# Three modulation pieces, one weight remainder and the reload of x in another place on their queues

## The reference

```python
def first_block(x, ...):
    a = rms_norm(h, g_mix_pre)
    proj = a @ w_in
    attn = moba_attention(q, k, v)
    conv = conformer_conv(u, b_glu, w_dw, b_dw, ln_g, ln_b)   # depthwise, layer_norm over channels, silu
    mixed = concatenate([attn, conv], axis=-1) @ w_out
    h = h + rms_norm(mixed, g_mix_post)
    f = rms_norm(h, g_ffn_pre)
    f = square(relu(f @ w_ff1)) @ w_ff2
    h = h + rms_norm(f, g_ffn_post)

def _modulation(cvec, w, b):          # w is 2048 x 6144: shift, scale, gate
    m = silu(cvec) @ w + b
```

## Time and profile before

| | |
|---|---|
| median of 3 runs | 1825.3 us (1824.86 to 1826.06) |
| the profiled execution | 1826.15 us, its span 1824.4 us |
| TensorE busy | 1802.3 us, 99% |
| VectorE busy | 1468.7 us, 81% |
| ScalarE busy | 902.9 us, 49% |
| granted TensorE clock, mean | 0.998 |
| moved by DMA | 426.92 MB, 234 GB/s |

### The profile page before, as it was taken

One profiled execution on the slowest core, in us unless ns is written; L12 is line 12 of the kernel. 1 busy time (PEld: TensorE's weight loads), 2 busy tenths in 40 slices (PEclk: granted clock), 3 DMA queues, 4 the chain that ended last, 5 costly groups with the idle time before them and its releaser, 6 DMA issues.

```text
span 1824.4 us, 26132 instructions
## 1 busy us (share of the span) xinstructions
PE 1802.3 (99%) x9884; PEld 1558.2 (85%) x9884; DVE 1468.7 (81%) x1709; ACT 902.9 (49%) x1176; POOL 112.9 (6%) x217
## 2 busy tenths in 40 slices
PE   8999999999999999999999999999999999999998
PEld 7899987888888888888888888888888888888986
DVE  6899998878888897889887888746788778897854
ACT  6444566555434433553454557423656545445443
POOL 0000000000000000000000000000111010000000
PEclk9999999999999999999999999999999999999999
DMA  8756447777786787778977964654666784878562
GB/s 324 257 175 199 153 155 289 260 242 270 255 286 232 256 291 233 246 260 290 253 246 264 319 226 162 230 185 140 230 199 216 266 289 149 272 247 278 195 218 106
DMA packets 191016, 426.92 MB, mean 234 GB/s; under 512 B 12480, under 2 KB 12864, under 8 KB 189760
## 3 DMA queue, kind: packets, MB, share of 16 engines
q1 hardware_dynamic: 158560, 323.74, 52.3%
q0 software_dynamic: 27648, 100.68, 16.6%
q10 hardware_dynamic: 4704, 1.07, 0.3%
HBM read 421.23 MB, written 4.21 MB: 233 GB/s over the span
## 4 chain that ended last, share of the span: by engine, by line
PE 93%; DVE 4%; ACT 1%; DMA 1%; issue 1%; DVEq 0%; SPq 0%; POOLq 0%; ACTq 0%
PE banks L2073 23%; PE banks L2118 14%; PE banks L2120 14%; PE banks L2119 14%; PE banks L2079 12%; PE banks L2064 4%; PE banks L2066 4%; PE banks L2065 4%; PE banks L2419 2%; PE banks L2435 2%; PE banks L2182 1%; PE banks L2410 1%; DMA mod_raw<-in_ev_mod_w 1%; DVE w_lo L1146 1%; DMA scratch<-in_x 0%
## 5 line engine op out<-in xcount | busy, mean ns | idle before, releaser
L550 ACT ACTIVATE w_hi<-raw 128x1024 fp32r<-128x1024 f32 x552 | 579.5, 1058 | 658.3 <-PE banks L2120 333.5
L1146 DVE TENSOR_TENSOR w_lo<-raw,w_hi 128x1024 fp32r<-128x1024 f32 x552 | 667.1, 1222 | 244.0 <-ACT w_hi L550 241.8
L2073 PE MATMUL banks<-a_pair,w_hi 128*128 128x512 f32 x1792 | 431.2, 391 | 1.5 <-DVE a_pair L1276 0.8
L2073 PEld LDWEIGHTS banks<-a_pair,w_hi 128*128 128x128 f32 x1792 | 328.3, 188 | 65.2 <-issue 2.0
L2118 PE MATMUL banks<-w_hi,b_hi 128*128 128x512 f32 x808 | 317.0, 392 | 2.9 <-DVE w_lo L1392 2.6
L2120 PE MATMUL banks<-w_hi,b_lo 128*128 128x512 f32 x808 | 315.1, 390 | 0.0
L2119 PE MATMUL banks<-w_lo,b_hi 128*128 128x512 f32 x808 | 315.1, 390 | 0.0
L1186 DVE SCALAR_TENSOR_TENSOR mod_sum<-mod_raw,silu_c,mod_sum 128x1024 f32<-128x1024 f32 x240 | 302.9, 1283 | 12.1 <-DMA mod_raw<-in_ev_mod_w 8.3
L2079 PEld LDWEIGHTS banks<-a_pair,w_lo 128*128 128x128 f32 x1792 | 230.2, 191 | 8.8
L2079 PE MATMUL banks<-a_pair,w_lo 128*128 128x256 f32 x1792 | 234.6, 283 | 0.0
L2118 PEld LDWEIGHTS banks<-w_hi,b_hi 128*128 128x128 f32 x808 | 152.1, 188 | 35.8 <-issue 3.9
(11 more groups left out here) (249 smaller groups left out, 1684.5 us busy)
## 6 DMA issues: line engine op xcount, KB each, us to landing
raw<-in_w_ff SPq DMA_DIRECT2D x128, 1024.0 KB, 6.5
mod_raw<-in_ev_mod_w POOLq DMA_DIRECT2D x96, 512.0 KB, 5.3
mod_raw<-in_od_mod_w POOLq DMA_DIRECT2D x96, 512.0 KB, 5.1
raw<-in_ev_w_in SPq DMA_DIRECT2D x40, 1024.0 KB, 5.1
raw<-in_w_in SPq DMA_DIRECT2D x39, 1024.0 KB, 5.1
raw<-in_od_w_in SPq DMA_DIRECT2D x32, 1024.0 KB, 6.4
raw<-in_w_out SPq DMA_DIRECT2D x16, 1024.0 KB, 5.4
raw<-in_ev_w_out SPq DMA_DIRECT2D x16, 1024.0 KB, 6.6
```

The costliest lines, as they stand in the source:

```text
L550: nc.scalar.activation(w_hi[:, s % SLOTS], raw[:, s // 2, KPS * (s % 2):KPS * (s % 2) + KPS, :], ACT.Copy).then_inc(hi_ready, 1)
L1146: nc.vector.tensor_tensor(w_lo[:, s % SLOTS], raw[:, s // 2, KPS * (s % 2):KPS * (s % 2) + KPS, :], w_hi[:, s % SLOTS].bitcast(F32), ALU.s ...
L2073: e = nc.tensor.matmul(out[:, f, :], w_hi[:, s % SLOTS, t, P * f:P * (f + 1)], rows[:, :, KPS * s + t, :], start=s == 0 and t == 0, stop=F ...
```

## The change

On VectorE's queue, pieces 8 and 9 of `ev_gate` no longer stand between the squares' sum and the variance, and piece 10 no longer stands behind the last channel tile. Pieces 8 to 11 now follow remainders 40, 41, 42 and 43; pieces 12 to 14 follow 45 to 47, 15 to 17 follow 49 to 51, and 18 to 20 follow 53 to 55. Before, pieces 11 and 12 followed 41 and 43, 13 and 14 followed 45 and 47, 15 and 16 followed 49 and 51, and 17 to 20 followed 52 to 55. The remainder 35 moves from behind the scaling to the place between reciprocal and scaling. On SP's queue the reload of x is issued behind unit 13 instead of unit 11. No instruction is added or removed.

```diff
@@ -404,7 +404,7 @@
-                if u == 11:
+                if u == 13:
                     sp.wait_ge(conv_ready, 8)
                     sp.dma_start(X, tok(io["x"])).then_inc(x_in, 16)
@@ -1456,15 +1456,14 @@
             channels_added(conv_sq, square_total)
-            halves("ev_gate", 8, 2)
             dve.wait_ge(ln_sum, 2)
             nc.vector.tensor_scalar(ln_rstd[:], ln_var, 1.0 / 1024, LN_EPS, ALU.mult, ALU.add).then_inc(ln_act, 1)
             ahead1(34)
             dve.wait_ge(conv_sq_ready, 2)
             link(nc.vector.reciprocal(ln_rstd[:], ln_rstd[:]))
+            ahead1(35)
             nc.vector.tensor_tensor(conv_y, conv_y, ln_rstd[:].unsqueeze(1).to_broadcast([P, CONV_TILES, T]),
                                     ALU.mult).then_inc(ln_act, 1)
-            ahead1(35)
             ahead1(36)
@@ -1472,7 +1471,6 @@
                 if k in (0, 2, 5):
                     ahead1({0: 37, 2: 38, 5: 39}[k])
-            halves("ev_gate", 10, 1)
@@ -1492,13 +1490,13 @@
             for i in range(3):
                 for f in range(40 + 4 * i, 44 + 4 * i):
                     ahead1(f)
-                    if f % 2:
-                        halves("ev_gate", 11 + 2 * i + f % 4 // 2, 1)
+                    if f == 40 or f % 4:
+                        halves("ev_gate", 8 + f - 40 - i, 1)
                 gained(2 * i, i, out_acc[i])
             for f in range(52, 58):
                 ahead1(f)
-                if f < 56:
-                    halves("ev_gate", 17 + f - 52, 1)
+                if 52 < f < 56:
+                    halves("ev_gate", 18 + f - 53, 1)
```

## The result

The changed kernel takes 1831.69 us (median of 7 runs, 1830.45 to 1833.84), the one before 1824.92 beside it (7 runs, 1824.57 to 1826.06). The ratio is 1.0038, with a 95% interval of 1.0027 to 1.0050: slower by 6.8 us. The profiled execution has 1831.19 us and a span of 1829.5, 5.1 more than the 1824.4 of before; it is one of the faster ones of this kernel, and that of before was, at 1826.15, above all seven of its own.

A forecast was written before the change was run, and what follows sets the result against it. Bound by VectorE's layer-norm chain, then modulation loads. Step 12's gain of 0.4 to 2.1 us is lost and the chain ends 5.9 us later: median 1825.3 becomes 1831.2, range of 8 in 10 1826.0 to 1836.5.

The forecast's parts named there:

- What bounds: Output product: VectorE's layer-norm chain to about 296, modulation loads from 300; chain and TensorE end within half a us.
- Parts 1 and 2: Layer norm: variance 1.53 us earlier, scaling only 0.38; wait moves from step 11 to 12, gaining 0.45 to 2.08 us.
- Part 3: Output product: pieces 8 to 10 behind the norm make six load periods of 8.32 us; piece 20 5.9 us later.
- the third rival: Load chain keeps the period of before, 9.3 us: piece 20 at 359.0, +11.8, time 1837.1; chance 0.14.
- Part 4: Reload of x two units later meets loads of pieces 13 and 14 instead; still one collision, no cost from x.
- TensorE's new waits: Output product: TensorE waits near steps 19 to 24 and before the last two; a slow clock there costs 1.6 us.
- The sum: Whole kernel: step 12's gain of 0.4 to 2.1 us lost, chain's end +5.9 us, median 1831.2.
- All lost: Output product: the 0.4 to 2.1 us gained at step 12 vanishes as TensorE waits again for remainders and the accumulator.
- the first rival: Loads keep up, landing under 5.4 us on average; TensorE sets the end: 1823.2, or 1824.9 with slow clock; chance 0.12.

## Why the prediction was right, point by point

- **What bounds.** Right. Both ends of the product, the chain's and TensorE's, had to be early for a gain; the kernel before with its chain relieved gained nothing. Of the two, the chain's is the one that sets the next product in the changed kernel, by 1.2 us (355.53 + 5.05 against 355.28 + 4.14).
- **Parts 1 and 2.** Right to 0.15 us at each step: scaling at 288.06 (287.95 forecast), channel 1 at 293.90 (293.8), step 12 at 294.38 (294.25) with a wait of 2.57 (2.65). The wait went one step on. The clock fell behind it, so of the two gains, 0.4 and 2.1, it was the smaller. The prediction had left open whether it would fall; what it had not foreseen is that the same wait leaves the clock up in other executions.
- **Part 3.** Right in mechanism, and two of its terms erred in opposite ways. Piece 8 at 303.43 (303.2) and piece 20 at 352.06 (353.1), six periods of 8.1 (8.32). But the six loads of this chain (pieces 10, 12, 14, 16, 18 and 20) took 4.4, 4.3, 6.8, 5.0, 6.7 and 5.2 us, 5.4 on average and not 6.4. The rest of the period, 4.6 us over the six, is VectorE's own order: a piece whose load has landed still stands behind other work. 3.4 us of it are at piece 12, whose load had landed at 316.1 while VectorE had just done piece 11, late for a load of 7.1 us, and had a gain product and two remainders to do. The forecast had this term at nothing and named it only for the third rival. Its 6.4 was the median of before; all 13 loads took 6.5 on average there and 5.9 here. In each kernel two of them met x (10.3 and 8.1 before, 8.3 and 6.8 here), so x explains at most a part of the difference, and why the others landed sooner stays open. That the sum came out so near is luck.
- **Part 4.** Right: x back at unit 11 and x alone at unit 13 show no difference that can be told. The load of piece 13 took 8.3 and that of 14 6.8, those that I had named. The load of piece 11, which I had put at 5.5 as free of x, took 7.1, and most of it had passed when x was issued at 312.7.
- **TensorE's new waits.** Forecast near steps 19 to 24 and before the last two; they were at steps 20, 23, 24 and 28, 3.5 us in all. The last one came at step 28, not before step 30.
- **The sum.** 5.9 forecast for the median, 6.8 measured, 5.1 between the two profiled executions, of which the chain gives 4.9. The 1.7 us between 6.8 and 5.1 are what one fall of the clock costs; the profiled execution of before had one and lies 1.2 above its median, so the median execution may have none, but no profile shows that. With 4.9 in place of 5.9 at piece 20, and this on top, the median came near the forecast by luck as well. "All lost" for the gain at step 12 was right for the changed kernel and too strong as a rule, as the run with remainder 35 back shows: that remainder delays the scaling by 1.1 us and with it the chain's start.
- **The rivals.** The run without loads is the first rival made real: TensorE ends at 348.6 as worked out. Its condition, landings under 5.4 on average, was all but met by the six loads of the chain (5.4), and still piece 20 was 4.9 us late. The condition was worked out without VectorE's order, and so was too mild.
- **The time of a transfer.** The Trainium skill, "DMA: Bandwidth & Descriptors", section "Anatomy of one DMA — SWDGE (gpsimd) path", would give 3.2 us for these loads, as an estimate. The shortest landing of this trace is 4.3 us and the middle one 5.3; the trace does not agree for these loads, which share the DMA engines with others, and the measurement decides.

## What to carry to other kernels

A transfer that is issued only when its buffer is read turns the reader's place in the program into a chain: count periods (use, issue, landing, and what stands before the next use), not instructions. Work moved off one critical stretch has to be looked at where it lands; here three pieces of 1.28 us each, moved behind a stage, cost some 7 us, while in places with an idle wait or a slack stage they cost nothing. And where an in-order engine feeds two consumers, moving one item ahead moves the wait to the other: ask which one is late next.

## What was not expected of the hardware

A wait of nearly the same length on TensorE is followed by the slow clock in one execution and not in the next. The idle time of TensorE was 2.16 us in the profiled execution of the kernel before, and the granted clock fell to 0.51; with 2.12 in the run with x alone and 2.16 in the kernel before with three pieces later it stayed at 1. With 2.57 it fell in the changed kernel, with 2.54 without loads it did not. Here are the same stretches without loads, where step 12 waits as in the changed kernel:

```profile
291.30:294.10 2.80, 0.26 (x2) 0.04 (x1) 2.04 (x4) 2.80 (x7) 0.00 (x0) 1.00 1.00 380
294.10:297.50 3.40, 3.40 (x15) 2.79 (x16) 2.46 (x5) 3.40 (x8) 0.00 (x0) 1.00 0.86 283
```

Fifteen matmuls are in these 3.4 us there, seven in the changed kernel. A fall costs about 1.7 us, as an estimate: half of the 3.4 us at half the clock. That is more than the differences that several of these edits were made for. Nor is a short wait safe: in the run with pieces and x moved the clock fell at 357.9, behind two waits of 1.28 and 0.74 us among the few short matmuls between the products. The Trainium skill, "TensorE: Matmul & The Clock Gate", section "HAM oscillation — how this bites in real kernels", says that waits between bursts bring the slow clock anew; these traces show it for some executions and not for others.
